# The sample caches are copied from GpSimd's queue in one-megabyte pieces, two in flight, where the sync engine's queue had carried them between its loads

## The reference

```
q, k, v, u = split(rmsnorm(x) @ w_in)           # 1024 -> 3 * 512 + 512
o_a = dilated sliding-window attention, 8 heads of 64   # samples: against cache_k_win, cache_v_win
o_b = multi-scale pooling of u
x  += concat(o_a, o_b) @ w_out
x  += cross attention, 4 heads of 256, 256 memory tokens  # samples: cache_mem_k, cache_mem_v
x  += top 4 of 32 experts, each 1024 -> 2 * 1024 -> 1024  # all weights float32
y   = rmsnorm(x)
k_win_sample = concat(cache_k_win, k)[:, 4:]     # the same for v: 8 samples x 2048 x 8 x 64
```

## Time and profile before

| | |
|---|---|
| Median of three runs | 1458.57 us |
| The profiled execution | 1459.92 us, span 1458.1 us |
| TensorE (PE) busy | 1290.5 us, 89% |
| VectorE (DVE) busy | 444.1 us, 30% |
| ScalarE (ACT) busy | 241.6 us, 17% |
| GpSimd (POOL) busy | 67.5 us, 5% |
| Moved by DMA | 562.84 MB, mean 386 GB/s |
| SP's queue | 557.16 MB |
| GpSimd's queue | 5.13 MB |

### The profile page before, as it was taken

How to read it: one execution, slowest core, us unless ns; L and a number is a source line. 1 busy time by engine, 2 the same in 40 slices (tenths; PEclk the granted TensorE clock), 3 DMA queues, 4 the chain that set the end, 5 groups by cost and what they waited for, 6 DMA issues and landing times.

```text
span 1458.1 us, 16691 instructions
## 1 busy us (share of the span) xinstructions
PE 1290.5 (89%) x6493; PEld 549.5 (38%) x6493; DVE 444.1 (30%) x999; ACT 241.6 (17%) x475; POOL 67.5 (5%) x69
## 2 busy tenths in 40 slices
PE   6994999898869799999999899989998999989986
PEld 4543443346644533333333233333333333333332
DVE  2216566523312631321321222212212222123124
ACT  1225443311321110110110010010010001001102
POOL 1010000000400700000000000000000000000000
PEclk9895988798987799999999999999999999999998
DMA  9999597799999679999999999999999999999994
GB/s 353 370 324 372 224 404 284 293 401 360 333 357 396 231 296 429 429 425 429 428 427 430 427 429 427 429 429 428 429 427 429 427 430 427 430 429 427 429 427 165
DMA packets 51213, 562.84 MB, mean 386 GB/s; under 512 B 6501, under 2 KB 8645, under 8 KB 20349
## 3 DMA queue, kind: packets, MB, share of 16 engines
q1 hardware_dynamic: 49589, 557.16, 93.6%
q0 software_dynamic: 1584, 5.13, 0.9%
HBM read 556.15 MB, written 73.28 MB: 432 GB/s over the span
## 4 chain that ended last, share of the span: by engine, by line
DMA 50%; PE 40%; DVE 6%; ACT 2%; issue 1%; SPq 0%; DVEq 0%; ACTq 0%
DMA wide<-in_w_gate_up 47%; PE bank L1901 11%; PE bank L1589 4%; PE bank L1568 3%; PE bank L1930 2%; PE bank L1696 2%; PE bank L1611 2%; DMA wide<-in_cache_k_win 2%; PE bank L1443 1%; PE bank L1488 1%; PE bank L1439 1%; DMA scr<-in_c_xdiag 1%; PE bank L1684 1%; PE bank L1641 1%; PE bank L1469 1%
## 5 line engine op out<-in xcount | busy, mean ns | idle before, releaser
L1901 PE MATMUL bank<-wide,att 128*64 128x512 f32 x2048 | 463.3, 596 | 59.0 <-DMA wide<-in_w_gate_up 58.8
L1901 PEld LDWEIGHTS bank<-wide,att 128*64 128x64 f32 x2048 | 139.3, 136 | 363.1 <-issue 228.6
L1930 PE MATMUL bank<-slim,att 128*64 128x512 f32 x1024 | 226.8, 595 | 0.0
L1375 DVE TENSOR_SCALAR att<-bank 128x512 f32<-128x512 f32 x32 | 22.1, 692 | 469.4 <-PE bank L1901 469.4
L1930 PEld LDWEIGHTS bank<-slim,att 128*64 128x64 f32 x1024 | 70.6, 137 | 152.2 <-issue 149.2
L1354 DVE TENSOR_TENSOR x<-x,bank 128x512 f32<-128x512 f32 x68 | 46.6, 686 | 233.2 <-PE bank L1883 226.5
L956 ACT ACTIVATE att<-att 128x512 f32<-128x512 f32 x32 | 20.2, 630 | 518.1 <-DVE att L1375 518.1
L1883 PE MATMUL bank<-tb,att 128*128 128x512 f32 (+1 forms) x192 | 84.7, 611 | 1.8 <-ACT tb L965 1.3
L965 ACT ACTIVATE tb<-bank 64x512 f32<-64x512 f32 x64 | 37.9, 592 | 234.1 <-PE bank L1930 233.7
L1589 PE MATMUL bank<-slim,ta 128*128 128x512 f32 x128 | 58.4, 610 | 0.0
L1850 PE MATMUL bank<-att,mkT 128*128 128x128 bf16 x408 | 46.5, 223 | 1.4 <-DVE att L1305 1.4
(11 more groups left out here) (282 smaller groups left out, 1183.1 us busy)
## 6 DMA issues: line engine op xcount, KB each, us to landing
wide<-in_w_gate_up SPq DMA_DIRECT2D x128, 2048.0 KB, 25.5
slim<-in_w_down SPq DMA_DIRECT2D x64, 2048.0 KB, 22.0
out_k_win_sample<-in_cache_k_win SPq DMA_DIRECT2D x16, 2044.0 KB, 25.9
out_v_win_sample<-in_cache_v_win SPq DMA_DIRECT2D x16, 2044.0 KB, 32.4
wide<-in_cache_k_win SPq DMA_DIRECT2D x16, 1024.0 KB, 11.3
wide<-in_cache_v_win SPq DMA_DIRECT2D x16, 1024.0 KB, 6.8
wide<-in_w_in SPq DMA_DIRECT2D x8, 1024.0 KB, 14.4
wide<-in_cache_mem_k SPq DMA_DIRECT2D x8, 1024.0 KB, 22.7
```

The costliest lines, as they stand in the source:

```text
L1901: ins = M(bk[half[h], :], rows[:, k, :], wide[:, k, c:c + 512], start=False, stop=k == KC - 1)
L1930: ins = M(bank_y[half[h], :], aT[:, f % 4, f // 4, :], slim[:, f, 512 * h:512 * h + 512], start=f == 0, stop=f == KC - 1)
```

## The change

The copies leave SP's list altogether. The pieces are halved: 64 of 1,046,528 bytes, 16 rows of 65,408 bytes. GpSimd issues them on its own queue in a new function `copies(n)`. They take two semaphores in turn, and piece n is only issued when piece n - 2 has landed, so that at most two are in flight and GpSimd stands still while it waits for one. GpSimd's program has them at these places: 10 when the second chunk of `w_in` has landed, 3 behind the stores of the bias table, 2 behind the stores of the prompt's keys and values, 1 behind each of the 16 small reductions, 12 behind the store of `mem_v_prompt`, 8 behind the split of the expert bias, and the 13 that remain behind the split of the activations. SP waits for all of them at its end.

```diff
-        COPIES = [6, 4, 2, 1, 0, 1, 1, 1, 2, 2, 5, 2, 2, 3]
...
+        moved_in = [sem("moved_in0"), sem("moved_in1")]
...
-                for h in range(2):
-                    pieces.append(tuple(ap.rearrange("s h d -> (s h d)").rearrange("(c a n) -> c a n", c=2, a=32)[h]
+                for h in range(4):
+                    pieces.append(tuple(ap.rearrange("s h d -> (s h d)").rearrange("(c a n) -> c a n", c=4, a=16)[h]
...
-            def copy(n):
-                for _ in range(n):
-                    dst, src = pieces.pop(0)
-                    sp.dma_start(dst, src).then_inc(stored["copies"], 16)
...
-            copy(COPIES.pop(0))
...
+            def copies(n):
+
+                for _ in range(n):
+                    lane = moved_in[moved[0] % 2]
+                    if moved[0] > 1:
+                        pool.wait_ge(lane, 16 * (moved[0] // 2))
+                    dst, src = pieces.pop(0)
+                    pool.dma_start(dst, src).then_inc(lane, 16)
+                    moved[0] += 1
+
+            pool.wait_ge(wide_in[1], 16)
+            copies(10)
             for h in range(HEADS):
                 read_out(pool, "toep", h)
...
+            copies(3)
...
+            copies(2)
             for b in range(DEC_B):
                 pool.wait_ge(scored, b + 1)
                 nc.gpsimd.partition_all_reduce(gm, mx, P, bass.bass_isa.ReduceOp.max).then_inc(gmax, 1)
+                copies(1)
                 pool.wait_ge(zpart, b + 1)
                 nc.gpsimd.partition_all_reduce(zz, zs, P, bass.bass_isa.ReduceOp.add).then_inc(zall, 1)
+                copies(1)
...
+            copies(12)
             for s in range(3):
                 pool.wait_ge(loaded[f"braw{s}"], 16)
...
+            copies(8)
             pool.wait_ge(parts_in, 1)
...
+            copies(len(pieces))
             pool.wait_ge(stored["kv"], 64)
```

More of the change, by code:

```diff
@@ L415, in build @@
         most_in = sem("most_in")
-        stored = {n: sem(f"stored_{n}") for n in ("copies", "kv", "pool", "mk", "mv", "y")}
+        stored = {n: sem(f"stored_{n}") for n in ("kv", "pool", "mk", "mv", "y")}
+        moved_in = [sem("moved_in0"), sem("moved_in1")]
         dve_done = sem("dve_done")
@@ L525, in _ @@
                     slim_round(ROUND_AT[b])
-                else:
-                    copy(COPIES.pop(0))
                 bb, use = place(("pv", b - 1))
@@ L553, in _ @@
                 cache_mem(cmem[b - 4], "cache_mem_k", b, ck_in[b - 4])
-                if b == 5:
-                    copy(COPIES.pop(0))
             for b in range(4, DEC_B):
@@ L606, in _ @@
             step0()
-            copy(len(pieces))
             with sp.Fori(1, EXPERTS) as e:
@@ L621, in _ @@
             sp.wait_ge(stored["y"], 48)
-            sp.wait_ge(stored["copies"], 16 * 4 * DEC_B)
+            sp.wait_ge(moved_in[0], 16 * 4 * DEC_B)
+            sp.wait_ge(moved_in[1], 16 * 4 * DEC_B)
         @block.gpsimd
@@ L638, in _ @@
                 pool.dma_start(gff[16 * a:16 * a + 16, :], gff_rows[a], allow_slow_non_contiguous=True).then_inc(gff_in, 16)
+            moved = [0]
+            def copies(n):
[8 more added lines that the diff above has]
+            copies(10)
             for h in range(HEADS):
```

## The result

The changed kernel is slower. Four runs took 1486.91, 1488.23, 1494.18 and 1497.77 us, median 1491.2, against 1458.67 for the kernel before; the ratio is 1.0228, 95% interval 1.0185 to 1.0271, which is clear of 1 and leaves open whether the loss is over 2%. The forecast was 1482.6 us, range 1464 to 1496, with 0.89 on slower. The profiled execution took 1486.91 us with a span of 1485.0, 26.9 more than before.

A forecast was written before the change was run, and what follows sets the result against it. From 518 us the end is set by DMA bytes, at 428 GB/s. Start and first window -2.0, `w_xv` +3, `w_xq` and `xdiag` 0, tail +23: +24 us on 1459.92, 1482.6 on the median's scale, range 1464 to 1496.

The forecast's parts named there:

- The tail: GpSimd's last 13 pieces, issued from 503.1 us: 8.8 remain on top of the full weight stream, costing 23 us.
- The line at 518 us: From 518 us to the end the DMA engines are full, so copy bytes moved behind that time add to the end.
- The start: Ten pieces beside `w_in`, one per 3.0 us, SP getting a fifth: sweep 5.5 us late, bounds 0 and 10.
- The case in which the loads stay ahead: Rival: SP has half or more of the engines beside copies, nothing is late; +8 us, 1466.6 us, chance 0.16.
- How an engine is shared: Beside `w_in`: a queue of small rows next to one of 65,408-byte rows is held well below half.
- the slow stores: Two 1.57 MB stores on GpSimd's queue beside six SP copies took 13.3 and 15.1 us, against 7.1 alone.
- First key window: Load VectorE and ScalarE wait for: there by 119 us, ahead of the engines; net 2.0 us gained, start delay included.
- `w_xv`: Load in the loop, behind two windows: two copy pieces now fall beside it, 3 us late, bounds 0 and 4.9.
- `w_xq`: Load issued at 326.46 us beside GpSimd's twelve pieces: a fifth of the engines until 338, 7 us late (0 to 10).
- `xdiag`: Load fed in with GpSimd's eight pieces: its wait stays and swallows that of `w_xq`; change 0, bounds -6 and +3.4.
- the rival of a faster second queue: Engines overlap copies and weights, the tail costs nothing and both waits go: 1440 us, chance 0.07.
- the 10 us by which the prediction said it would be wrong: Sign of error: TensorE's first expert matmul moving by more than 10 us.

The follow-up runs named there:

- the second profile: The changed kernel run once more, unaltered: first expert matmul at 526.9 us, experts' stage 938.2 us, median 1498.99 us, ratio 1.0246.
- the first move alone: The kernel before, with 3 pieces of 2.09 MB moved from ahead of the first windows to behind them, on SP's queue: 1457.24 us, ratio 0.9973.

## Why the prediction was right, point by point

- **The tail.** Forecast 23 us (19.0 to 28.7); measured 21.3 in the stage, and 21.4 when the 13 pieces were left out. The price per piece was near weights' speed, as taken.
- **The line at 518 us.** Held in all runs: a piece that is through before the experts start costs nothing there (13 on SP: 916.5), one behind it costs about its bytes.
- **The start.** This step failed. I took a piece every 3.0 us and a fifth of the engines for SP, so the last chunk of `w_in` near 54 us and the sweep 5.5 us late. The chunk landed at 48.4, and the sweep ended at 54.6, earlier than before by 1.4. From the third to the tenth piece it was 21.46 to 51.37 us, one per 4.3 us, for a piece landed in 8 to 9 us and not in 5.8 (lines below), and SP got 36% of the bytes. The case in which the loads stay ahead was right here.
- **How an engine is shared.** I had read from the slow stores that a queue of small rows beside one of 65,408-byte rows gets well below half. Both shares above bear that out. The Trainium skill ("DMA: Bandwidth & Descriptors", "Queues, rings and completion order") has packets of 9 to 17 descriptors alternate, by which four in flight should have harmed little. With four in flight SP sent two 8,192-byte rows for each row of a copy, not nine or more, and the sweep came 14.4 us later. By the Trainium skill ("DMA: Bandwidth & Descriptors", "Anatomy of one DMA") a transfer on this queue takes 2.0 us + bytes / 436e3, an estimate of 4.4 us for a piece; the fastest landing here was 5.1.
- **First key window.** Forecast -2.0 net with bounds of -7.5 and +2.6. The sweep was not late, VectorE and ScalarE no longer stand for the window, and the late-key turn came 9.8 us earlier (117.9 against 127.7), outside the bounds. TensorE still waits 7.1 us there, now for ScalarE, which has its own work to finish first.
- **`w_xv`.** Forecast +3 (0 to 4.9). TensorE's sixteen matmuls on line 1593 that start at 173.71 started at 182.79 before; those behind `w_xv` start at 220.89, and at 225.23 before. So of 9.1 us of lead 4.3 are left, 5.0 when line 1572 begins, with `w_xv` in the chain. Of the 9.8 us, 4.8 were lost in the loop, within the bounds here; in the second profile all 8.3 were. A rival is open: with the first move alone, and all copies on SP's queue, the loop loses as much, with a value window in the chain.
- **`w_xq`.** Forecast 7 us (0 to 10); its matmuls took 13.4 longer. Mis-sized: the twelve pieces lasted from 297.95 to their last issue at 343.75, not to 338. SP's share was not too small: it moved 3.13 of 8.38 MB in 326 to 346 us, over a third and not a fifth.
- **`xdiag`.** Forecast 0 (-6 to +3.4); it came 7.0 us later, outside its bounds. Right was that the wait does not go and is fed by GpSimd's eight pieces: without them the load lands in 4.1 us. Wrong was that it swallows the wait for `w_xq`. TensorE comes 8.4 us late out of the matmuls on `w_xq` (383.1 against 374.7), it is still 8.4 us late at line 1776 (1772 before, 421.47), and SP issues `xdiag` only then: at 430.01, and at 421.63 before. The load takes 14.6 us where it had taken 16.0, so 7.0 of the 8.4 us come through (lines below).
- **How fast two queues go together.** Against the rival of a faster second queue the prediction sets 425 GB/s "with both queues at work" in 125 to 143 us. That is a misreading: GpSimd's queue moved 0.01 MB there, and the mixture was copies and loads on SP's queue. The changed kernel shows the rate with both at work: 392 GB/s in 395 to 430 us, no more than with one.
- **The sum.** +24 forecast, +26.9 in the profiled span. Ahead of the experts I had +1.0 and it was +5.6: 7.8 better at the first window (-9.8 for -2.0), 1.8 worse in the loop, 12.0 worse from the output projection to `xdiag` (from -5.0 to +7.0, for 0), and 1.4 given back behind it. The tail was 1.7 better. The near hit of the sum is in part luck: errors of both signs cancel, and the profiled execution was the fastest of its four. The second profile has +14.2 ahead of the experts, beyond the 10 us by which the prediction said it would be wrong, +22.9 in the stage and +37 in all; the profiles without the tail and with the tail on SP's queue have +15.3 and +15.4 ahead of the experts. The median, 32.5 us above that of before, lies between. The tail stands in every run; the part ahead of the experts was forecast near zero and is mostly not.

The two lines of `xdiag` in the chain of the kernel before and at TensorE in the changed one (start us, us, what):

```profile
421.63 15.97 DMA scr<-in_c_xdiag
```

```profile
429.84 7.07 PE L1776 MATMUL bank<-wide,att 128*32 128x512 f32 x64
```

The landing times behind the third and fourth point, of the pieces of the value caches and of the key caches in the changed kernel (the line of the issues, and the time from issue to landing over all of that name, shortest, median, longest):

```profile
L632 POOL DMA_DIRECT2D out_v_win_sample<-in_cache_v_win x32: 488/488/720, 29.5 to 557.3; - x32
...
DMA to landing us min/median/max: 5.6/8.1/18.1
L632 POOL DMA_DIRECT2D out_k_win_sample<-in_cache_k_win x32: 488/488/720, 13.7 to 538.1; - x32
...
DMA to landing us min/median/max: 5.1/7.8/10.9
```

## What to carry to other kernels

Where the last stage is bound by bytes, every transfer that nothing waits for must be through before that stage starts; ask of a moved one on which side of that line it falls, and in which idle stretch of the DMA engines it can ride. A wait for a load that stands behind bulk copies in one queue is cured by its place in that queue; a second queue does not order the two, it lets them share, and the loads' share depends on how long the other queue stays full. An engine that computes can issue only when its own work lets it, and its waits for transfers delay that work (4.5 us with seven pieces in the split); where a sequencer that computes nothing has room in its list, bulk transfers are better issued there. And a load that is issued on a signal from compute inherits every delay of that compute: it cannot hide one.

## What the runs showed of the hardware

Two queues do not share the DMA engines evenly by bytes: with four 1 MB pieces of 65,408-byte rows in flight SP's queue of 8,192-byte rows got 1.43 of 7.64 MB in 20 to 40 us, about two of its rows for each row of a copy, and TensorE waited 11.1 us for `w_in`; with two in flight it got 2.94 of 8.19 MB and TensorE never waited for `w_in`. Two profiles of the changed kernel differ by 8.6 us ahead of the experts and by 1.6 in them. In the first series the kernel before kept within 1.2 us over four runs and the changed one within 11; in the later series the kernel before itself ranged over 6 and 13 us in 17 runs each, so I do not call this a property of the second queue.
